# Sums of squares moved inside the first step of the next product, in three places of a two-block float32 network

## The chip, the cores and the metric

One core of one Trainium2 chip runs the whole program in one launch. The metric is the device time of one execution in microseconds (us); the median of several executions is compared.

## What is computed

The reference is two small transformer-like blocks, one after the other, on 512 tokens of width 1024, all in float32. Only the first block matters here. Its two layers each end in the same feed-forward part, and the second layer begins with a query projection:

```python
def rms_norm(x, g, eps=NORM_EPS):
    xf = x.astype(jnp.float32)
    y = xf * lax.rsqrt(jnp.mean(xf * xf, axis=-1, keepdims=True) + eps)
    return (y * g.astype(jnp.float32)).astype(x.dtype)

def swiglu_ffn(h, w_gu, w_down):
    gate, up = jnp.split(h @ w_gu, 2, axis=-1)
    return (jax.nn.silu(gate) * up) @ w_down
...
        h = rms_norm(x, g_ffn[layer])
        x = x + swiglu_ffn(h, ffn_w_gu[layer], ffn_w_down[layer])
```

The hidden width is 2816, that is 22 tiles of 128. Since the norm's factor is one number for each token, it can be multiplied in after the product: `(x*g) @ w` is formed from the residual stream x at once, and the factor 1/sqrt(mean(x*x) + eps) is needed only where the product's result is taken out of PSUM.

## The kernel before, in words

**Products.** x lies transposed, as 8 tiles of 128 features by 512 tokens. A float32 product is done as three matmuls in the type float32r: high part times high part, low times high, high times low (`three`, lines 2479 to 2481). The kernel works through a list of steps. A step of a product with 8 input tiles makes 256 output features in two PSUM banks with 8 x 2 x 3 = 48 matmuls of 128x128 by 512. Each step reads one weight slot of 128x2048 numbers. Slots go through two buffers by turns: SyncE fetches the raw weights (`fill`, two DMAs for a slot, let go when the low part of the slot two before it is done), ScalarE copies them to the type float32r (`high`, line 1220, `w_hi`), GpSimd subtracts to get the low part (`low`, line 1099, `w_lo`), in 8 pieces of 256 columns or, with `cut=False`, in one instruction. `high(n)` waits until the step that used slot n-2 is over.

**A product's input.** For each of the 8 tiles k VectorE multiplies x by the norm's gain into one of two buffers `xf` (L1800), ScalarE copies it to `X_hi` (L1242, `x_high1`), VectorE subtracts to get `X_lo` (L1773). The first step of the product waits at tile k for `X_lo` of tile k.

**Sums of squares.** Ahead of three products whose input is normed (gu0, q, gu1) ScalarE squares the 8 tiles of x into two buffers by turns (`norm_squares`, L1283), and TensorE sums over partitions by a plain float32 matmul with a 128x128 matrix of ones (`norm_sum`, L2555), which the profile shows as two passes for each tile. Square k waits for the sum of tile k-2. Before, all eight sums stand on TensorE ahead of the first step of the product. After the last of them ScalarE takes the root (L1285, `rt`) and VectorE the reciprocal (L1788).

**gu0 and gu1** (gate and up) have 22 steps each, written as a loop of 11 iterations with 2 steps, on each engine its own loop. When a step is over VectorE scales the two banks by `rt` (L1822, L1823), ScalarE applies Silu (L1205), VectorE multiplies (L1826), ScalarE copies the result to `hb_hi` (L1207), VectorE subtracts to get `hb_lo` (L1829). In ScalarE's loop (`ffn`) each step begins with `high` of the slot of the next step, then comes Silu and the copy of the step itself. In GpSimd's loop (`low_ffn`) the low parts are uncut. The loops of dn0 and dn1 (4 steps with 22 input tiles and 3 slots each) follow; on ScalarE they hold copies alone.

**q** has 4 steps in straight-line code. Beside its later steps TensorE does small matmuls for the heads, put between input tiles by a function `parts(k)` that `features` calls ahead of tile k: rotations of queries (L2859) and head sums (L2850). The first of them stands in step 1 ahead of tile 2 and needs step 0 scaled (`aq`, L2167), and VectorE waits for the table `rope` before it does that (L2210). SyncE issues the DMA of `rope` (L1051) after the fills of all four q slots. The fourth fill waits for the low part of the second slot.

**Order.** All orders are written out by hand, one instruction stream for each engine, tied by semaphores. TensorE works strictly in the order of its stream.

Of the kernel before, what the change touches and what calls it, by code (L numbers as in the profile page):

```python
# [19 lines left out]
ACT = mybir.ActivationFunctionType  # L20
# [5 lines left out]
KT = D // P  # L26
TT = S // P
F = 2816
FT = F // P
# [171 lines left out]
PL = make_plan()  # L201
# [372 lines left out]
def build(nc, t, out):  # L574
# [3 lines left out]
    with ctx:  # L578
# [25 lines left out]
        xf = sb("xf", [P, 2, S])  # L604
# [242 lines left out]
        def bank(i, n=S):  # L847
            return psum[:, i, 0:n]
# [4 lines left out]
        def wait_done(eng, key):  # L853

            eng.wait_ge(job_done, JB.info[key][2] + 1)
# [30 lines left out]
        def c_(name, n=P, o=0):  # L886
            return cst[:, CST[name] + o:CST[name] + o + n]
# [32 lines left out]
        def square_buffer(i):  # L920

            return (xf[:, :, :], pt8[:, 6:8, :], sgate[:, :, :], tq2[:, :, :])[i]
# [161 lines left out]
        def _(pool):  # L1084
# [24 lines left out]

            def low_ffn(layer):  # L1110
                n0 = PL.first_slot[f"gu{layer}"]
                with pool.Fori(0, FT // 2) as i:
                    for j in range(2):
                        low(n0 + j, 2 * i, cut=False)
                n0 = PL.first_slot[f"dn{layer}"]
                with pool.Fori(0, 2) as i:
                    for j in range(6):
                        low(n0 + j, 6 * i, cut=False)
# [71 lines left out]
        def _(act):  # L1190
# [7 lines left out]

            def ffn(layer):
                s0, n0 = PL.first[f"gu{layer}"], PL.first_slot[f"gu{layer}"]  # L1200
                with act.Fori(0, FT // 2) as i:
                    for j in range(2):
                        high(n0 + j + 1, 32 * i, 16 * i)
                        act.wait_ge(ff_raw, FT * layer + j + 1 + 2 * i)
                        act.activation(sgate[:, j, :], sgate[:, j, :], ACT.Silu).then_inc(ff_gate, 1)  # L1205
                        act.wait_ge(ff_prod, FT * layer + j + 1 + 2 * i)
                        act.activation(hb_hi[:, bass.ds(2 * i + j, 1), :], xf[:, j:j + 1, :],  # L1207
                                       ACT.Copy).then_inc(ff_hi, 1)
                n0 = PL.first_slot[f"dn{layer}"]
                with act.Fori(0, 2) as i:  # L1210
                    for j in range(6):
                        high(n0 + j + 1, 96 * i, 44 * i)
# [20 lines left out]
            def x_high1(v, k, src=None):  # L1233
                if src is None:
                    act.wait_ge(xf_ready, xf_count(v, k))
                if v:
                    act.wait_ge(kstep, xv_last_k(v - 1, k))
                if src is None:
                    f = mixed_at(k) if v < XV["y"] else xf[:, k % 2, :]
                else:  # L1240
                    f = src[:, k, :]
                act.activation(X_hi[:, k, :], f, ACT.Copy).then_inc(xhi_ready, 1)  # L1242
# [24 lines left out]
                    if after is not None:  # L1267
                        after(k)

            def norm_squares(i, v=None):  # L1270

                for k in range(0 if v is None else 6):
                    x_high1(v, k)
                for k in range(KT):
                    if k >= 6 and v is not None:
                        x_high1(v, k)
                    if i == 0:
                        wait_job(act, ("xt", k))
                    elif k % 2 == 0:
                        wait_step(act, PL.first[("", "o", "dn0", "ao")[i]] + k // 2)  # L1280
                    if k >= 2:
                        act.wait_ge(sq_used, 7 * i + k - 1)
                    act.activation(square_buffer(i)[:, k % 2, :], x[:, k, :], ACT.Square).then_inc(sq_ready, 1)  # L1283
                wait_done(act, ("rms", i))
                act.activation(rt[:, :], bank(6), ACT.Sqrt, bias=cst[:, C_EPS6:C_EPS6 + 1],  # L1285
                               scale=1.0 / D).then_inc(job_a, 1)
# [260 lines left out]
            for i in range(4):  # L1547
                if PL.first_slot["o"] + 1 + i < len(PL.slots):
                    high(PL.first_slot["o"] + 1 + i)
            norm_squares(1, XV["ffn0"])  # L1550
            ffn(0)
            act.wait_ge(lam_row, 1)
            wait_done(act, ("lam",))
            act.activation(col[:, 0:2], psum[:, 7, 0:2], ACT.Exp).then_inc(job_a, 1)
            norm_squares(2, XV["qin"])
            rq, rk = xf[0:16, 1, :], xf[0:16, 0, :]

            def qk_part(n):
# [19 lines left out]
                        act.activation(n_hi[:, :], rk, ACT.Copy).then_inc(kn_h, 1)  # L1578

            for n in range(72):  # L1580
                if n % 8 == 0:
                    next_slot(PL.first["q"] + n // 8)
                if n == 24:
                    x_high(XV["kvin"])
                qk_part(n)
# [14 lines left out]
            for p in range(N_UNITS + 2):  # L1600
                j = p // PER_STEP
# [38 lines left out]
                x_high1(XV["attn"], k, oT)  # L1640
            for i in range(PL.count["ao"]):
                next_slot(PL.first["ao"] + i)
            norm_squares(3, XV["ffn1"])
            ffn(1)

            for k in range(KT):
# [820 lines left out]
        def _(pe):  # L2467
            order = [0]

            def begin(key):  # L2470
                assert JB.order[order[0]] == key, (JB.order[order[0]], key)
                order[0] += 1
                wait_banks(pe, key)
                return job_banks(key)[0]
# [39 lines left out]
            def ffn(layer):  # L2514

                s0, v = PL.first[f"gu{layer}"], XV[f"ffn{layer}"]
                with pe.Fori(0, FT // 2) as i:
                    for j in range(2):
                        pe.wait_ge(step_d, PL.taken[s0 + j][1] - 2 + 2 * i)
                        features(s0 + j, v if j == 0 else None, dyn=2 * i, check=False)  # L2520
                s0 = PL.first[f"dn{layer}"]
                with pe.Fori(0, 2) as i:
                    for j in range(2):
                        pe.wait_ge(step_d, PL.taken[s0 + j][1] - 2 + 2 * i)
                        features(s0 + j, None, hb_hi, hb_lo, dyn=6 * i, check=False,
                                 tile_ready=(ff_lo, FT * layer) if j == 0 else None)
# [21 lines left out]
                for i in range(PL.count[name]):  # L2548
                    (kind or features)(PL.first[name] + i, v if i == 0 else None)

            def norm_sum(i):
                begin(("rms", i))
                for k in range(KT):
                    pe.wait_ge(sq_ready, 8 * i + k + 1)
                    ins = pe.matmul(bank(6), c_("ones"), square_buffer(i)[:, k % 2, :], start=k == 0, stop=k == KT - 1)  # L2555
                    ins.then_inc(sq_used if k < KT - 1 else job_done, 1)

            pe.wait_ge(cst_in, 16)
            for k in range(KT):
# [2 lines left out]
                for tt in range(TT):  # L2562
                    ins = pe.transpose(psum[:, b, P * tt:P * tt + P], xtok[:, tt, P * k:P * k + P], c_("ident"))
                ins.then_inc(job_done, 1)
            norm_sum(0)
            pe.wait_ge(rows_in, 16 * (len(ROWS_A) + len(ROWS_B) + 2))
            b = begin(("pv",))
            pe.transpose(psum[:, b, 0:P], prow[0][:, :], c_("ident"))
# [241 lines left out]
            for k in range(KT):  # L2810
# [8 lines left out]
                if k % 2 == 0:  # L2819
# [4 lines left out]
                    for m in range(2):  # L2824
# [5 lines left out]
                                    (sg_hi[96:128, 1, :], sg_lo[96:128, 1, :]), False, True)  # L2830
                    ins.then_inc(kstep, 1)
            product("o", XV["y"])
            norm_sum(1)
            ffn(0)
            pe.wait_ge(lam_row, 1)
            b = begin(("lam",))
            pe.matmul(psum[:, b, 0:2], cst[0:1, CST["ones"]:CST["ones"] + P], col[0:1, 14:16], start=True,
                      stop=True).then_inc(job_done, 1)
            norm_sum(2)

            def qk_part(n):
                for what, w, i in QK_AT.get(n, ()):
# [32 lines left out]
                two(bank(b), heads_r[:, P * k:P * k + P], (n_hi[:, :], n_lo[:, :])).then_inc(job_done, 1)  # L2875

            for i in range(4):
                features(PL.first["q"] + i, XV["qin"] if i == 0 else None, parts=lambda k: qk_part(8 * i + k))
            pe.wait_ge(rt_ready, 3)
            b = begin(("rtT",))  # L2880
            for tt in range(TT):
# [106 lines left out]
                b = begin(("oinv", k))  # L2988
                two(bank(b), heads_r[:, P * k:P * k + P], (n_hi[:, :], n_lo[:, :])).then_inc(job_done, 1)
            product("ao", XV["attn"])  # L2990
            norm_sum(3)
            ffn(1)
            def to_tokens(n, k):

# [203 lines left out]
```

## Time and profile before

| | us |
|---|---|
| median of three executions | 2226.78 (2226.38 to 2231.42) |
| the profiled execution, its own time | 2220.09 |
| its span, from the first to the last instruction | 2218.3 |
| TensorE busy (PE) | 2005.0, 90% |
| VectorE (DVE), ScalarE (ACT), GpSimd (POOL) busy | 792.4, 812.1, 777.7 |
| low parts of the weights on GpSimd, 588 instructions | 706.1 |
| mean granted TensorE clock | 0.948 of 2.4 GHz |

The profile calls the engines PE (TensorE's matmuls), PEld (its weight loads, which overlap), DVE, ACT, POOL and SP. Shares of busy time are means over stages with different limits. Matmuls are pipelined, so two that follow each other overlap in the rows, and a stream is best read by the distance from one start to the next.

### The profile page before, as it was taken

To read this page: it belongs to the slowest core of one execution; us is meant where nothing else is said; L and a number is where in the kernel's file an instruction comes from. 1 tells how busy PE (TensorE), PEld (TensorE's weight loads), DVE (VectorE), ACT (ScalarE), POOL (GpSimd) and SP (SyncE) were. 2 spreads that over 40 slices of the span, in tenths; PEclk is the share of its full clock that TensorE was granted. 3 is DMA by queue.
4 is the path that set the end of the run, shared out by engine and by line. 5 is a ranking of instruction groups with operands and counts; after the bars stand their busy time and mean duration, and the time that the engine had idled before them with its cause. 6 is when DMAs were issued, how large, how long until landed. Compare 5 with 4: busy or idle time off the path is not lost.

```text
span 2218.3 us, 37433 instructions
## 1 busy us (share of the span) xinstructions
PE 2005.0 (90%) x15948; PEld 1570.5 (71%) x15948; DVE 792.4 (36%) x1248; ACT 812.1 (37%) x1061; POOL 777.7 (35%) x644
## 2 busy tenths in 40 slices
PE   5997976668999999989999899999999999979987
PEld 3666866643778888866667478888887886768767
DVE  5586443324332221014766632222102223324333
ACT  6766133332244343122247534343312423242232
POOL 3353322210334443433432034444444433234432
PEclk8998999986899999999999899999999999989988
DMA  5111000010223333222121022333223121131211
GB/s 154 57 50 63 2 5 5 4 48 23 59 75 94 99 90 109 95 80 67 65 69 39 0 76 76 97 92 102 97 91 106 60 77 57 39 100 58 77 38 58
DMA packets 190138, 147.16 MB, mean 66 GB/s; under 512 B 6826, under 2 KB 188289, under 8 KB 190004
## 3 DMA queue, kind: packets, MB, share of 16 engines
q1 hardware_dynamic: 190004, 145.18, 21.2%
q8 instruction: 107, 1.75, 0.3%
q14 instruction: 27, 0.22, 0.0%
HBM read 143.07 MB, written 2.10 MB: 65 GB/s over the span
## 4 chain that ended last, share of the span: by engine, by line
PE 79%; DVE 7%; ACT 5%; issue 5%; POOL 2%; DMA 1%; SPq 0%; DVEq 0%; ACTq 0%
PE psum L2479 21%; PE psum L2481 20%; PE psum L2480 20%; PE psum L2634 4%; POOL w_lo L1099 2%; ACT w_hi L1220 1%; DVE X_lo L1773 1%; PE psum L2555 1%; PE psum L2485 1%; PE psum L2859 1%; PE psum L2920 1%; PE psum L2933 1%; PE psum L2850 1%; PE psum L3030 1%; DVE col L2230 0%
## 5 line engine op out<-in xcount | busy, mean ns | idle before, releaser
L1099 POOL TENSOR_TENSOR w_lo<-weight_raw,w_hi 128x256 fp32r<-128x256 f32 (+5 forms) x588 | 706.1, 1233 | 1236.5 <-ACT w_hi L1220 1236.4
L2479 PE MATMUL psum<-X_hi,w_hi 128*128 128x512 f32 x1400 | 577.4, 412 | 26.3 <-DVE X_lo L1773 17.8
L2481 PE MATMUL psum<-X_hi,w_lo 128*128 128x512 f32 x1400 | 552.3, 395 | 0.0
L2480 PE MATMUL psum<-X_lo,w_hi 128*128 128x512 f32 x1400 | 551.9, 394 | 0.0
L1220 ACT ACTIVATE w_hi<-weight_raw 128x2048 fp32r<-128x2048 f32 (+2 forms) x134 | 249.5, 1862 | 362.9 <-PE psum L2481 338.3
L2479 PEld LDWEIGHTS psum<-X_hi,w_hi 128*128 128x128 f32 x1400 | 266.5, 190 | 126.8 <-issue 53.8
L2480 PEld LDWEIGHTS psum<-X_lo,w_hi 128*128 128x128 f32 x1400 | 266.8, 191 | 58.7 <-issue 7.5
L2481 PEld LDWEIGHTS psum<-X_hi,w_lo 128*128 128x128 f32 x1400 | 266.3, 190 | 58.1
L2479 PE MATMUL psum<-w_hi,X_hi 128*128 128x256 f32 x640 | 191.4, 299 | 13.0 <-DVE X_lo L1773 10.8
L2480 PE MATMUL psum<-w_lo,X_hi 128*128 128x256 f32 x640 | 185.1, 289 | 0.0
L2481 PE MATMUL psum<-w_hi,X_lo 128*128 128x256 f32 x640 | 184.9, 289 | 0.0
L1822 DVE TENSOR_TENSOR sgate<-rt,psum 128x512 f32<-128x512 f32 x44 | 30.3, 688 | 320.5 <-PE psum L2481 320.5
L2479 PEld LDWEIGHTS psum<-w_hi,X_hi 128*128 128x128 f32 x640 | 127.2, 199 | 21.0 <-issue 19.0
L2479 PE MATMUL psum<-hb_hi,w_hi 128*128 128x512 f32 x352 | 136.9, 389 | 0.0
L2480 PE MATMUL psum<-hb_lo,w_hi 128*128 128x512 f32 x352 | 136.9, 389 | 0.0
L2481 PE MATMUL psum<-hb_hi,w_lo 128*128 128x512 f32 x352 | 136.9, 389 | 0.0
L2480 PEld LDWEIGHTS psum<-w_lo,X_hi 128*128 128x128 f32 x640 | 127.0, 198 | 0.6 <-issue 0.5
L2481 PEld LDWEIGHTS psum<-w_hi,X_lo 128*128 128x128 f32 x640 | 126.7, 198 | 0.0
L1205 ACT ACTIVATE sgate<-sgate 128x512 f32<-128x512 f32 x44 | 27.9, 634 | 255.3 <-DVE sgate L1822 255.3
L1812 DVE TENSOR_TENSOR x<-x,psum 128x512 f32<-128x512 f32 x32 | 20.5, 682 | 224.6 <-PE psum L2481 224.6
L2480 PEld LDWEIGHTS psum<-hb_lo,w_hi 128*128 128x128 f32 x352 | 66.1, 188 | 13.8
L2481 PEld LDWEIGHTS psum<-hb_hi,w_lo 128*128 128x128 f32 x352 | 66.1, 188 | 13.8
(465 smaller groups left out, 2566.3 us busy)
## 6 DMA issues: line engine op xcount, KB each, us to landing
weight_raw<-in_ffn_w_gu SPq DMA_DIRECT2D x88, 512.0 KB, 4.8
weight_raw<-in_l_w_in SPq DMA_DIRECT2D x45, 512.0 KB, 4.7
weight_raw<-in_ffn_w_down SPq DMA_DIRECT2D x40, 512.0 KB, 3.6
weight_raw<-in_kv_w SPq DMA_DIRECT2D x16, 512.0 KB, 4.5
weight_raw<-in_l_w_out SPq DMA_DIRECT2D x16, 512.0 KB, 4.5
weight_raw<-in_rw_w_k SPq DMA_DIRECT2D x8, 512.0 KB, 6.6
weight_raw<-in_rw_w_r SPq DMA_DIRECT2D x8, 512.0 KB, 4.0
weight_raw<-in_rw_w_v SPq DMA_DIRECT2D x8, 512.0 KB, 4.0
```

Of the source, the lines that this page charges most:

```text
L1099: ins = pool.tensor_tensor(l, r, h.bitcast(F32), ALU.subtract)
L1205: act.activation(sgate[:, j, :], sgate[:, j, :], ACT.Silu).then_inc(ff_gate, 1)
L1220: last = act.activation(h, r, ACT.Copy)
L1773: dve.tensor_tensor(X_lo[:, k, :], f, X_hi[:, k, :].bitcast(F32), ALU.subtract).then_inc(xlo_ready, 1)
L1822: dve.tensor_tensor(sgate[:, j, :], rt[:, :], bank(b[0]), ALU.mult).then_inc(ff_raw, 1)
L2479: pe.matmul(ps, wh, xh, start=start, stop=False, skip_group_check=True)
L2480: pe.matmul(ps, wh, xl, start=False, stop=False, skip_group_check=True)
L2481: return pe.matmul(ps, wl, xh, start=False, stop=stop, skip_group_check=True)
L2485: pe.matmul(ps, w, xx[0], start=True, stop=False, skip_group_check=True)
L2555: ins = pe.matmul(bank(6), c_("ones"), square_buffer(i)[:, k % 2, :], start=k == 0, stop=k == KT - 1)
L2634: ins = pe.matmul(out(q, r, k), left(q, r, k), right(q, r, k), start=True, stop=True, skip_group_check=True)
L2850: ins = pe.matmul(psum[0:16, job_banks(key)[0], :], c_("sel64", 16, 16 * i), oT[:, i, :], start=i == first, stop=i == last)
```

## The change

In all three places (gu0, q, gu1) the eight sums leave their place ahead of the product. `features` gets them as `parts` of the first step: ahead of input tile k (k from 1) TensorE does the sum of tile k-1, and ahead of tile 7 those of tiles 6 and 7. On ScalarE squares and copies of input tiles take turns from the first tile on (before, six copies came first), and the copy `high` of the product's second weight slot moves from behind the root to between square 5 and tile 6. For that the first two steps of gu0 and gu1 are taken out of the loops of TensorE, ScalarE and GpSimd and written straight, the loops run from 1 to 10, and the low parts of these two slots are done in pieces. VectorE's loop stays as it is. The diff:

```diff
             def low_ffn(layer):
                 n0 = PL.first_slot[f"gu{layer}"]
-                with pool.Fori(0, FT // 2) as i:
+                low(n0)
+                low(n0 + 1)
+                with pool.Fori(1, FT // 2) as i:
                     for j in range(2):
                         low(n0 + j, 2 * i, cut=False)
...
-                with act.Fori(0, FT // 2) as i:
+
+                def hidden(j, at_, dyn):
+                    act.wait_ge(ff_raw, FT * layer + j + 1 + dyn)
+                    act.activation(sgate[:, j, :], sgate[:, j, :], ACT.Silu).then_inc(ff_gate, 1)
+                    act.wait_ge(ff_prod, FT * layer + j + 1 + dyn)
+                    act.activation(hb_hi[:, at_, :], xf[:, j:j + 1, :], ACT.Copy).then_inc(ff_hi, 1)
+
+                hidden(0, slice(0, 1), 0)
+                high(n0 + 2)
+                hidden(1, slice(1, 2), 0)
+                with act.Fori(1, FT // 2) as i:
                     for j in range(2):
                         high(n0 + j + 1, 32 * i, 16 * i)
-                        act.wait_ge(ff_raw, FT * layer + j + 1 + 2 * i)
...
+                        hidden(j, bass.ds(2 * i + j, 1), 2 * i)
...
-            def norm_squares(i, v=None):
-
-                for k in range(0 if v is None else 6):
-                    x_high1(v, k)
+            def norm_squares(i, v=None, early=None):
+
                 for k in range(KT):
-                    if k >= 6 and v is not None:
+                    if v is not None:
                         x_high1(v, k)
...
+                    if k == 5 and early is not None:
+                        high(early)
...
-            norm_squares(1, XV["ffn0"])
+            norm_squares(1, XV["ffn0"], PL.first_slot["gu0"] + 1)
...
-            norm_squares(2, XV["qin"])
+            norm_squares(2, XV["qin"], PL.first_slot["q"] + 1)
...
-                if n % 8 == 0:
+                if n % 8 == 0 and n:
                     next_slot(PL.first["q"] + n // 8)
...
-                with pe.Fori(0, FT // 2) as i:
+                pe.wait_ge(step_d, PL.taken[s0][1] - 2)
+                features(s0, v, check=False, parts=norm_beside(1 + 2 * layer))
+                pe.wait_ge(step_d, PL.taken[s0 + 1][1] - 2)
+                features(s0 + 1, check=False)
+                with pe.Fori(1, FT // 2) as i:
...
+            def norm_part(i, k):
+
+                if k == 0:
+                    begin(("rms", i))
+                pe.wait_ge(sq_ready, 8 * i + k + 1)
+                pe.matmul(bank(6), c_("ones"), square_buffer(i)[:, k % 2, :], start=k == 0, stop=k == KT - 1
+                          ).then_inc(sq_used if k < KT - 1 else job_done, 1)
+
+            def norm_beside(i):
+
+                def part(k):
+                    if k:
+                        norm_part(i, k - 1)
+                    if k == KT - 1:
+                        norm_part(i, k)
+                return part
...
-                features(PL.first["q"] + i, XV["qin"] if i == 0 else None, parts=lambda k: qk_part(8 * i + k))
+                features(PL.first["q"] + i, XV["qin"] if i == 0 else None,
+                         parts=norm_beside(2) if i == 0 else lambda k: qk_part(8 * i + k))
```

The calls `norm_sum(1)`, `norm_sum(2)` and `norm_sum(3)` are gone.

## Rows read from the trace of the kernel before

**Rows 1.** The page's part 4: the chain that ended last, by engine
```profile
PE 79%; DVE 7%; ACT 5%; issue 5%; POOL 2%; DMA 1%; SPq 0%; DVEq 0%; ACTq 0%
```

**Rows 2.** Timeline of PE before gu0: start, length, line, tiles [idle before <-releaser]
```profile
611.92 0.39 PE L2481 MATMUL psum<-X_hi,w_lo 128*128 128x512 f32 x1
613.91 7.85 PE L2555 MATMUL psum<-pt,cst 128*128 128x512 f32 x16 [1.60 <-ACT pt L1283]
...
621.83 0.40 PE L2480 MATMUL psum<-X_lo,w_hi 128*128 128x512 f32 x1
```

**Rows 3.** Timeline of DVE at the start of gu0
```profile
622.52 3.35 DVE L1788 RECIPROCAL rt<-rt 128x512 f32<-128x512 f32 x1 [1.73 <-ACT rt L1285]
632.70 0.69 DVE L1822 TENSOR_TENSOR sgate<-rt,psum 128x512 f32<-128x512 f32 x1 [6.83 <-PE psum L2481]
...
654.46 0.69 DVE L1822 TENSOR_TENSOR sgate<-rt,psum 128x512 f32<-128x512 f32 x1 [7.17 <-PE psum L2481]
...
665.61 0.69 DVE L1822 TENSOR_TENSOR sgate<-rt,psum 128x512 f32<-128x512 f32 x1 [7.45 <-PE psum L2481]
```

**Rows 4.** Waits in gu0 and dn0, 615 to 990: total, times, longest (us)
```profile
PEld psum L2479 <- POOL w_lo L1099: 4.0, 10, 0.4
```

**Rows 5.** Timeline of ACT at the start of gu0
```profile
621.79 0.69 ACT L1285 ACTIVATE rt<-psum,cst 128x512 f32<-128x512 f32 x1 [1.22 <-PE psum L2555]
...
646.46 1.28 ACT L1220 ACT_TABLE_LOAD   x1
```

**Rows 6.** Timeline of POOL in gu0: low parts of slots 2 and 3
```profile
637.47 4.59 POOL L1099 TENSOR_TENSOR w_lo<-weight_raw,w_hi 128x2048 fp32r<-128x2048 f32 x1 [7.07 <-ACT w_hi L1220]
649.75 4.60 POOL L1099 TENSOR_TENSOR w_lo<-weight_raw,w_hi 128x2048 fp32r<-128x2048 f32 x1 [7.68 <-ACT w_hi L1220]
```

**Rows 7.** Timeline of PE between dn0 and q
```profile
983.48 0.38 PE L2837 MATMUL psum<-col,cst 1*128 1x2 f32 x2
991.86 10.44 PE L2555 MATMUL psum<-sgate,cst 128*128 128x512 f32 x16 [8.00 <-ACT sgate L1283]
```

**Rows 8.** Timeline of DVE between dn0 and q
```profile
985.96 0.69 DVE L1773 TENSOR_TENSOR X_lo<-xf,X_hi 128x512 fp32r<-128x512 f32 x1 [30.09 <-ACT X_hi L1242]
...
1018.46 1.28 DVE L2167 TENSOR_TENSOR aq<-rt,psum 128x512 f32<-128x512 f32 x2 [9.79 <-DMA rope<-c_rope]
```

**Rows 9.** Timeline of ACT between dn0 and q: copy of q's second slot
```profile
1003.02 1.91 ACT L1220 ACTIVATE w_hi<-weight_raw 128x2048 fp32r<-128x2048 f32 x1
```

**Rows 10.** Timeline of POOL between dn0 and q: low part of that slot
```profile
1005.01 5.59 POOL L1099 TENSOR_TENSOR w_lo<-weight_raw,w_hi 128x256 fp32r<-128x256 f32 x8 [21.99 <-ACT w_hi L1220]
```

**Rows 11.** Timeline of PE in q: a 128x128 float32 matmul between a step's matmuls
```profile
1037.16 0.40 PE L2481 MATMUL psum<-X_hi,w_lo 128*128 128x512 f32 x1
1037.39 1.02 PE L2859 MATMUL psum<-aq,rotg 128*128 128x512 f32 x2
...
1038.49 0.39 PE L2480 MATMUL psum<-X_lo,w_hi 128*128 128x512 f32 x1
```

**Rows 12.** Timeline of PE in q: a 128x16 float32 matmul between a step's matmuls
```profile
1041.66 0.40 PE L2481 MATMUL psum<-X_hi,w_lo 128*128 128x512 f32 x1
...
1043.29 0.40 PE L2480 MATMUL psum<-X_lo,w_hi 128*128 128x512 f32 x1
```

**Rows 13.** ACT by line in gu0's loop, 621 to 866: busy, mean ns
```profile
L1220 ACT ACT_TABLE_LOAD x11 | 14.1, 1283 | 0.2
L1205 ACT ACT_TABLE_LOAD x11 | 14.1, 1283 | 0.2
```

**Rows 14.** ACT by line in dn0's loop, 866 to 983, its first group
```profile
L1220 ACT ACTIVATE w_hi<-weight_raw 128x2048 fp32r<-128x2048 f32 (+1 forms) x12 | 21.3, 1774 | 89.4 <-PE psum L2481 89.4
```

**Rows 15.** Stretches: length, PE, PEld, DVE, ACT, POOL, granted clock, DMA, GB/s
```profile
987.40:997.60 10.20, 5.74 (x7) 2.42 (x8) 6.39 (x12) 4.81 (x9) 0.00 (x0) 0.50 0.00 1
1693.70:1696.10 2.40, 0.03 (x1) 0.06 (x1) 2.05 (x3) 0.00 (x0) 2.12 (x3) 1.00 0.00 0
...
1697.30:1700.70 3.40, 3.40 (x10) 2.63 (x9) 0.00 (x0) 0.00 (x0) 0.00 (x0) 0.50 0.91 294
```

More of the change, by code:

```diff
@@ L1200, in ffn @@
                 s0, n0 = PL.first[f"gu{layer}"], PL.first_slot[f"gu{layer}"]
-                with act.Fori(0, FT // 2) as i:
+                def hidden(j, at_, dyn):
[7 more added lines that the diff above has]
+                with act.Fori(1, FT // 2) as i:
                     for j in range(2):
                         high(n0 + j + 1, 32 * i, 16 * i)
-                        act.wait_ge(ff_raw, FT * layer + j + 1 + 2 * i)
[L1205 to L1208, printed above, removed]
+                        hidden(j, bass.ds(2 * i + j, 1), 2 * i)
                 n0 = PL.first_slot[f"dn{layer}"]
@@ L1642, in _ @@
                 next_slot(PL.first["ao"] + i)
-            norm_squares(3, XV["ffn1"])
+            norm_squares(3, XV["ffn1"], PL.first_slot["gu1"] + 1)
             ffn(1)
@@ L2516, in ffn @@
                 s0, v = PL.first[f"gu{layer}"], XV[f"ffn{layer}"]
-                with pe.Fori(0, FT // 2) as i:
+                pe.wait_ge(step_d, PL.taken[s0][1] - 2)
[3 more added lines that the diff above has]
+                with pe.Fori(1, FT // 2) as i:
                     for j in range(2):
                         pe.wait_ge(step_d, PL.taken[s0 + j][1] - 2 + 2 * i)
-                        features(s0 + j, v if j == 0 else None, dyn=2 * i, check=False)
+                        features(s0 + j, dyn=2 * i, check=False)
                 s0 = PL.first[f"dn{layer}"]
@@ L2549, in product @@
                     (kind or features)(PL.first[name] + i, v if i == 0 else None)
[L2551 to L2556, printed above, removed]
+            def norm_part(i, k):
[11 more added lines that the diff above has]
+                return part
             pe.wait_ge(cst_in, 16)
@@ L2564, in _ @@
                 ins.then_inc(job_done, 1)
-            norm_sum(0)
+            for k in range(KT):
+                norm_part(0, k)
             pe.wait_ge(rows_in, 16 * (len(ROWS_A) + len(ROWS_B) + 2))
@@ L2832, in _ @@
             product("o", XV["y"])
-            norm_sum(1)
             ffn(0)
@@ L2838, in _ @@
                       stop=True).then_inc(job_done, 1)
-            norm_sum(2)
             def qk_part(n):
@@ L2990, in _ @@
             product("ao", XV["attn"])
-            norm_sum(3)
             ffn(1)
```

## The prediction, on record before the change was run

> **What bounds the kernel now.** I read the chain that ended last first: TensorE holds 79% of it [rows 1], so a change pays where TensorE stands still or does work that could lie elsewhere. Then its timeline around the three places. Ahead of gu0 the last matmul of the product before starts at 611.92, the sums follow after 1.60 us of idling, and the first step runs from 621.6 (its second matmul starts at 621.83, one spacing of 0.23 after that) [rows 2]. The place ahead of gu1 looks the same to within 0.1 us. A step is 10.88 us long: VectorE takes out step 0 at 632.70 and step 2 at 654.46, two steps later [rows 3]; so a tile of 6 matmuls is 1.36 and a spacing 0.227. Inside gu0 each second step starts late: 665.61 to 654.46 is 11.15, that is 0.27 more, and the waits show TensorE held 10 times by the low part of a weight slot [rows 4]. Between dn0 and q TensorE stands for 8.00 us and then does the sums in 10.44 [rows 7]; but what q then waits for is the table rope: VectorE starts on step 0's result at 1018.46, after idling 9.79 for that DMA [rows 8]. So three stages have three different limits, and each part below is costed at its own.
>
> **A sum inside a step.** The sums are not removed, they are put between tiles. The nearest row is a float32 matmul of the same shape (128x128 weights, 512 columns) already between float32r matmuls: 1037.16 to 1038.49 is 1.33, less two spacings, 0.88 [rows 11]. With 16 weight columns it is 1.63 less 0.45, 1.18 [rows 12]. I take 0.88, the row of the same shape, and keep 1.18 as the upper bound. Nothing cheaper is seen: in the block each took (621.60 - 613.91)/8 = 0.96, with waits for squares among it [rows 2].
>
> **gu0 and gu1.** Step 0 then starts right behind the last matmul, at 612.15, and ends 10.88 + 8 x 0.88 = 17.9 later, at 630.05; before, 621.6 + 10.88 = 632.48. That is 2.4 gained for TensorE. But the norm's factor comes later against the step: the eighth sum is done one tile before the end, at 628.69. Root and reciprocal follow as before (the root starts 0.19 behind the sum and takes 0.69 [rows 5], the reciprocal 3.35 [rows 3]): 632.96. With about 0.1 for entering VectorE's loop, which was covered until now, step 0 is taken out from 633.06, against 632.70 before. This is the new wait: behind it hang, in order, Silu, the copy to `hb_hi`, ScalarE's copy of slot 2, which stands behind them in its stream, and GpSimd's low part of slot 2, and step 2 needs that. From taking out to the end of the low part was 632.70 to 642.06, 9.36 [rows 3, 6]. So the low part ends at 642.42 and step 2 starts 0.16 later (as step 3 did behind the low part ending at 654.35 [rows 6], 654.51 being 665.61 less 10.88 and the 0.22 from a step's end to its taking out). Step 2: 642.58, before 643.36. Of 2.4 only 0.8 is left there. At step 3, before 654.51 and now 642.58 + 10.88 = 653.46, it is 1.05, since its low part is no longer last.
>
> **Table loads in the loop.** Before, each of the 11 iterations on ScalarE loads an activation table twice, ahead of the first copy and ahead of Silu, 1283 ns each [rows 13], although the second half of an iteration copies behind Silu with no load. In dn0's loop, entered from Silu's table and holding only copies, there is none [rows 14]. What differs is that gu0's loop is entered behind a root and repeated behind Silu, dn0's always behind Silu. I read this as: a load stands where the ways in bring different tables. With the first two steps written straight, the loop is entered behind Silu as well, and I expect its 20 loads to go, one load for Silu staying ahead of step 0, under the reciprocal. The load at the loop's head (646.46 [rows 5]) lies on the path to the odd slots: 654.46 less 10.88 is 643.58, and from there to 654.35 it is 10.77, as against 9.36 without. Without it the low part comes 1.3 earlier than needed, and 9 further waits of 0.27 go: 2.4. For each of gu0 and gu1 1.05 + 2.4 = 3.5, together 7.0.
>
> The Trainium skill says otherwise ("ScalarE activation tables: per-element evaluation and per-set limits", section "Table sets in the compiler and the runtime"): "The back end places the table loads per block: greedy longest run". By that a loop's body starts over and would keep a load at its head. The rows speak against it twice, two loads in one body and none in the other. By this rule the gain of this part would be the first 1.05 each.
>
> **q.** TensorE is free at 983.86 [rows 7], the first `X_lo` is there at 986.65 [rows 8], so step 0 starts at 986.7, 2.8 us behind. After such a gap the clock may fall: behind an idle stretch of 2.40 us the granted clock was 0.50, 1.2 GHz, for 3.40 us, while the matmuls already ran [rows 15]. I take the same here, a loss of 1.7; both ends are kept, none and twice that. The fourth sum ends 4 x (1.36 + 0.88) = 8.95 later, with the loss at 997.35; square 5 waits for it, and behind that square ScalarE copies q's second slot, at 998.1. Before it was 1003.02 [rows 9]: 4.9 earlier. The low part follows in 5.59 [rows 10]; two `X_lo` now fall beside it, for which I allow 0.2, so 4.7. Behind the low part SyncE lets go the fourth fill and then rope, both issued by the same queue and landing as before; so step 0 is taken out 4.7 earlier, at 1013.8, and with it all of q. The factor is no limit there: eighth sum at 1004.9, with root, reciprocal and 2.2 us of small VectorE work 1011.4. Step 0 itself ends at 1006.3, 6.7 us earlier than before, and TensorE waits ahead of the first rotation longer than before: most of that goes into this wait.
>
> **Edits costed at nothing.** Two slots' low parts in pieces take 5.6 and not 4.6 each. The first ends near 609.1, before step 0 needs it at 612.15. The second starts behind the early copy at 623.8 and ends at 629.4 to 629.9 with two `X_lo` between; step 1 needs it at 630.05, and the wait of 1.65 at step 2 covers what is late. Tile 6 of x is copied behind the early copy: `X_lo` at 625.1, needed at 625.57; without this slack of 0.5 each tenth late moves the factor and step 2. A square waits for the sum two tiles back and the next tile's copy waits behind it, 2.1 us in all, while TensorE needs 4.5 for two tiles and sums: covered twice over. SyncE's fills are let go earlier, never later.
>
> **Sum.** 7.0 + 4.7 = 11.7. The profiled execution of 2220.1 would become 2208.4. It is 6.7 below the median of 2226.8, from which I take the same off: **2215.1**.
>
> **Rivals.**
> The loads stay in the loop. For it speaks only that I infer the rule from two loops. Gain 2 x 1.05 + 4.7 = 6.8, time 2220.0. Chance 0.13.
> A sum costs 1.18. Each of gu0 and gu1 loses 8 x 0.3 = 2.4 on the way to step 2 and keeps 1.1; q loses 4 x 0.3 and keeps 3.5. Gain 5.7, time 2221.1. Chance 0.10.
> The clock stays high in q. TensorE starts at 986.7, and 1.7 more comes back: 2213.4. Chance 0.12.
> Slower: the clock stays low through q's first step, as it did for 10.2 us around the sums before [rows 15], in which TensorE stood half the time. The eighth sum then ends 16.5 later than in my sum without a loss, at 1019.8, the factor and the small work at 1026.2, not rope, decide, and q loses 7.7 against before, more than the 7.0 won elsewhere: 2227.5. It decides from 31.5 us of low clock on, where half of that puts the factor 7.0 behind 1018.46. Against it: in a stream without holes 3.4 us were enough to come back [rows 15]. Chance 0.05.
>
> **How the numbers follow.** The forecast has 0.57, and 0.03 is left for what I don't see, taken as slower. Bounds: 2213.4 with the clock high, 2221.1 with dear sums; executions of one kernel differ by 1 to 2, so the range is 2212 to 2222. About 0.3%, 6.7 us, is what a measurement here can tell from no change. Faster by more: nearly all of the forecast (0.54), all of the high clock (0.12), half of the loads' rival (0.07): 0.73. Within it: the rest of the forecast, the other half, dear sums, and most of the low clock: 0.23. Slower: 0.04.
>
> **What would show it.** Right: no PE rows of L2555 in one block; in gu0 step 0 taken out near 633 less the shift, step 2 a wait of some 1.7 behind `w_lo`, no further waits of 0.27, and one table load, not 22, for each of gu0 and gu1 on L1205 and L1220; in q `aq` still behind rope, and some 30 us, not 34.6, behind the end of TensorE's last matmul of that stretch, `lam` (L2837, 983.86). Wrong: loads at L1220 in the loop; a sum of over 1 us between tiles; `aq` behind the factor; a low clock after q's first step has begun for more than 7 us.

## The result and the profile after

The changed kernel took 2217.25 us (median of 14 runs, 2212.15 to 2224.65), the kernel before, run beside it on the same chips, 2228.3 (14 runs, 2222.28 to 2238.35). The ratio is 0.9943, with a 95% interval of 0.9929 to 0.9957: about 12.7 us, or 0.57%, faster (the two medians by themselves differ by 11.05). The forecast was a gain of 11.7 and a time of 2215.1.

The profiled execution of after took 2218.33 us with a span of 2216.2, only 1.8 less than the one of before. That is no contradiction: the two executions also differ where the code does not. I cut each span at events that both have, VectorE's residual adds and the first `aq`, and took the differences of their starts:

| stretch, us | before | after | less |
|---|---|---|---|
| start to the residual add of step 2 of the product before gu0 | 601.47 | 613.48 | -12.01 |
| from there to the same add in dn0 (gu0, dn0) | 352.21 | 348.71 | 3.50 |
| from there to the first `aq` (q's first step) | 64.78 | 59.69 | 5.09 |
| from there to the add of step 2 ahead of gu1 | 292.72 | 290.39 | 2.33 |
| from there to the same add in dn1 (gu1, dn1) | 352.61 | 348.72 | 3.89 |
| from there to the end | 554.52 | 555.24 | -0.72 |

Rows two, three and five hold the change: 12.5 together. The first row is not the change's: over all profiled executions of both kernels and of the experiments that stretch lay between 600.9 and 616.75, with the same code. So the whole time says little of a few microseconds, and the stretches say much: the same kernel profiled again gave 348.69, 59.79, 290.57 and 348.71 for the four in the middle. The experiments below are read by these stretches, with the whole time beside them.

The page of after, its part 1 and its chain of work by engine (for [rows 1]): TensorE's busy time fell from 2005.0 to 1993.2 for the same 15948 matmuls (the mean granted clock was 0.954 and not 0.948, and busy time times clock is the same to 0.1%, so that fall needs no other cause), ScalarE's from 812.1 to 754.3, which is 42 table loads of 1.28 and a little more, and GpSimd has 28 instructions more.

```profile
PE 1993.2 (90%) x15948; PEld 1570.1 (71%) x15948; DVE 790.1 (36%) x1248; ACT 754.3 (34%) x1019; POOL 786.9 (36%) x672
...
PE 75%; issue 7%; DVE 7%; ACT 5%; POOL 4%; DMA 1%; SPq 0%; DVEq 0%; ACTq 0%; POOLq 0%
```

**gu0.** In after the lines stand 8 lower (L1830 is the old L1822, L1228 the old L1220). Times of after are 12.01 later than those of before up to this point. TensorE's timeline, where [rows 2] had one block of sums: start, length, line, tiles, [idle before, releaser].

```profile
625.29 0.39 PE L2489 MATMUL psum<-X_hi,w_lo 128*128 128x512 f32 x1
625.52 1.02 PE L2568 MATMUL psum<-pt,cst 128*128 128x512 f32 x2
...
626.60 0.39 PE L2488 MATMUL psum<-X_lo,w_hi 128*128 128x512 f32 x1
...
642.43 0.47 PE L2487 MATMUL psum<-X_hi,w_hi 128*128 128x512 f32 x1 [0.20 <-POOL w_lo L1099]
...
654.50 0.50 PE L2487 MATMUL psum<-X_hi,w_hi 128*128 128x512 f32 x1 [0.90 <-POOL w_lo L1099]
```

The sum lies between two tiles of step 0. Step 1 starts at 642.43 and step 2 at 654.50, each behind a low part. VectorE's timeline there, for [rows 3], shows what followed: the reciprocal, then step 0 to step 4 taken out.

```profile
641.61 3.35 DVE L1796 RECIPROCAL rt<-rt 128x512 f32<-128x512 f32 x1 [3.37 <-ACT rt L1293]
645.18 0.69 DVE L1830 TENSOR_TENSOR sgate<-rt,psum 128x512 f32<-128x512 f32 x1 [0.23 <-DVE rt L1796]
...
653.64 0.69 DVE L1830 TENSOR_TENSOR sgate<-rt,psum 128x512 f32<-128x512 f32 x1 [4.82 <-PE psum L2489]
...
665.71 0.69 DVE L1830 TENSOR_TENSOR sgate<-rt,psum 128x512 f32<-128x512 f32 x1 [8.46 <-PE psum L2489]
...
676.59 0.69 DVE L1830 TENSOR_TENSOR sgate<-rt,psum 128x512 f32<-128x512 f32 x1 [7.17 <-PE psum L2489]
...
687.47 0.69 DVE L1830 TENSOR_TENSOR sgate<-rt,psum 128x512 f32<-128x512 f32 x1 [7.17 <-PE psum L2489]
```

From step 2 on every step is 10.88 long; the 0.27 at each second one is gone. Of the ten waits for a low part of [rows 4] these are left, in the view of waits in gu0 and dn0, 627 to 990 (total, times, longest); they are the starts of steps 1 and 2 just shown:

```profile
PEld psum L2487 <- POOL w_lo L1099: 1.3, 1, 1.3
PE psum L2487 <- POOL w_lo L1099: 1.1, 2, 0.9
```

ScalarE's timeline and GpSimd's, for [rows 5] and [rows 6]: the early copy, root, the one table load, copy of slot 2; low parts of slots 0, 1 and 2.

```profile
633.84 1.90 ACT L1228 ACTIVATE w_hi<-weight_raw 128x2048 fp32r<-128x2048 f32 x1
...
640.88 0.69 ACT L1293 ACTIVATE rt<-psum,cst 128x512 f32<-128x512 f32 x1 [2.46 <-PE psum L2568]
641.59 1.28 ACT L1206 ACT_TABLE_LOAD   x1
...
647.87 1.90 ACT L1228 ACTIVATE w_hi<-weight_raw 128x2048 fp32r<-128x2048 f32 x1
...
615.53 7.52 POOL L1099 TENSOR_TENSOR w_lo<-weight_raw,w_hi 128x256 fp32r<-128x256 f32 x8 [5.29 <-ACT w_hi L1228]
635.81 6.47 POOL L1099 TENSOR_TENSOR w_lo<-weight_raw,w_hi 128x256 fp32r<-128x256 f32 x8 [12.76 <-ACT w_hi L1228]
649.85 4.59 POOL L1099 TENSOR_TENSOR w_lo<-weight_raw,w_hi 128x2048 fp32r<-128x2048 f32 x1 [7.57 <-ACT w_hi L1228]
```

**q.** The timelines of PE, ACT, POOL, SP and DVE in the order of the chain (for [rows 7] to [rows 10]): the end of `lam`, TensorE's start, the copy of q's second slot, its low part, the DMA of rope, the first `aq`, TensorE's first rotation.

```profile
992.00 0.38 PE L2859 MATMUL psum<-col,cst 1*128 1x2 f32 x2
995.32 0.48 PE L2487 MATMUL psum<-X_hi,w_hi 128*128 128x512 f32 x1 [2.94 <-DVE X_lo L1781]
...
1006.73 1.90 ACT L1228 ACTIVATE w_hi<-weight_raw 128x2048 fp32r<-128x2048 f32 x1
...
1008.70 6.47 POOL L1099 TENSOR_TENSOR w_lo<-weight_raw,w_hi 128x256 fp32r<-128x256 f32 x8 [17.16 <-ACT w_hi L1228]
...
1016.16 0.50 SPq L1051 DMA_DIRECT2D rope<-c_rope  x1
...
1021.88 1.28 DVE L2175 TENSOR_TENSOR aq<-rt,psum 128x512 f32<-128x512 f32 x2 [2.42 <-issue]
...
1023.22 1.22 PE L2880 MATMUL psum<-aq,rotg 128*128 128x512 f32 x1 [4.92 <-DVE aq L2175]
```

`lam` ends at 992.38, and `aq` starts 29.50 behind it; before it was 1018.46 less 983.86, 34.60. For the wait of 2.42 ahead of `aq` this profile names no releaser. That it is rope follows from the experiments: `aq` comes 5.7 to 5.9 behind the issue of rope in every run that has it in this place (6.87 in the one profile of before), and 2.4 earlier when rope is issued sooner.

### The profile page after: what moved, and what is told of

The parts are those of the page before. It is cut to its first block, busy times and chain, and to the rows that moved or that the text cites. A ratio compares the mean times of both kernels' runs of the same rounds, so it can differ in the third digit from the quotient of the medians.

```text
span 2216.2 us, 37365 instructions
## 1 busy us (share of the span) xinstructions
PE 1993.2 (90%) x15948; PEld 1570.1 (71%) x15948; DVE 790.1 (36%) x1248; ACT 754.3 (34%) x1019; POOL 786.9 (36%) x672
## 4 chain that ended last, share of the span: by engine, by line
PE 75%; issue 7%; DVE 7%; ACT 5%; POOL 4%; DMA 1%; SPq 0%; DVEq 0%; ACTq 0%; POOLq 0%
PE psum L2487 20%; PE psum L2489 19%; PE psum L2488 19%; PE psum L2657 4%; POOL w_lo L1099 4%; ACT w_hi L1228 2%; DVE X_lo L1781 1%; PE psum L2493 1%; PE psum L2942 1%; PE psum L2880 1%; PE psum L2955 1%; PE psum L2871 1%; PE psum L3051 1%; DVE col L2238 0%; PE psum L2494 0%
## 5 line engine op out<-in xcount | busy, mean ns | idle before, releaser
L1099 POOL TENSOR_TENSOR w_lo<-weight_raw,w_hi 128x256 fp32r<-128x256 f32 (+4 forms) x616 | 715.3, 1192 | 1215.9 <-ACT w_hi L1228 1215.7
L1228 ACT ACTIVATE w_hi<-weight_raw 128x2048 fp32r<-128x2048 f32 (+2 forms) x134 | 249.2, 1860 | 355.8 <-PE psum L2489 329.8
L1830 DVE TENSOR_TENSOR sgate<-rt,psum 128x512 f32<-128x512 f32 x44 | 30.2, 687 | 299.3 <-PE psum L2489 298.9
L2487 PEld LDWEIGHTS psum<-hb_hi,w_hi 128*128 128x128 f32 x352 | 66.1, 188 | 13.8
```

Source lines behind the costliest of these rows:

```text
L1099: ins = pool.tensor_tensor(l, r, h.bitcast(F32), ALU.subtract)
L1228: last = act.activation(h, r, ACT.Copy)
L1830: dve.tensor_tensor(sgate[:, j, :], rt[:, :], bank(b[0]), ALU.mult).then_inc(ff_raw, 1)
L2487: pe.matmul(ps, wh, xh, start=start, stop=False, skip_group_check=True)
```

## The experiments

**A Silu ahead of the loop, in the kernel before.** My theory was that a table load stands in ScalarE's loop only because the loop is entered behind a root and repeated behind Silu. If so, a single activation of Silu ahead of the unchanged loop must take the loads out of it; by the rival each body keeps its loads. The edit, for gu0 and gu1:

```diff
+                act.activation(ypart[:, 0:1], cst[:, C_EPS6:C_EPS6 + 1], ACT.Silu)
                 with act.Fori(0, FT // 2) as i:
```

> The kernel before with one Silu on a column of 128 numbers ahead of ScalarE's loop of gu0 and of gu1, nothing else; it makes both ways into the loop bring Silu's table. Theory (a load stands where the ways in bring different tables): of 44 loads in the two loops none is left, one for Silu stays ahead of each; the 10 late starts of 0.27 us in each of gu0 and gu1 go, 5.4 us in all, ratio to before 0.9976. Rival (loads are placed for each loop body from new): 11 or 22 loads stay in each loop, the late starts stay, ratio 1.000.

Measured: 2222.09 us, ratio 0.9967 (0.9943 to 0.9991). The stretch with gu0 took 349.47 (before 352.21), that with gu1 349.51 (before 352.61): 2.7 and 3.1 less. ScalarE by line in gu0, 620 to 870, for [rows 13]:

```profile
L1206 ACT ACTIVATE sgate<-sgate 128x512 f32<-128x512 f32 x21 | 13.3, 634 | 146.2 <-DVE sgate L1823 146.2
...
L1201 ACT ACT_TABLE_LOAD x1 | 1.3, 1283 | 0.0
```

One load, at the new line; of the 22 in the loop none is left, and with them went all of TensorE's waits for low parts in gu0. One instruction of 0.2 us does what I had put down to the steps written straight.

**A root ahead of the loop, in the changed kernel.** The reverse: the loop from 1 to 10 is entered behind a root again.

```diff
+                act.activation(ypart[:, 0:1], cst[:, C_EPS6:C_EPS6 + 1], ACT.Sqrt)
                 with act.Fori(1, FT // 2) as i:
```

> The changed kernel with one square root on a column of 128 numbers ahead of ScalarE's loop of gu0 and of gu1, so that the ways in bring different tables again. Theory: 20 loads come back on each of the two lines in each loop pair (10 iterations, 2 loads), the 9 or 10 late starts of 0.27 in each loop come back, about 5.2 us lost against the changed kernel, ratio to before 0.9966. Rival (the gain does not hang on the loads): ratio as the changed kernel's, 0.9943.

Measured: 2220.75 us, ratio to before 0.9961 (0.9943 to 0.998). The stretches grew by 2.94 and 3.31 against after, 6.2 together; 5.2 were expected. ScalarE by line, 612 to 866, and TensorE's waits, 612 to 975:

```profile
L1206 ACT ACT_TABLE_LOAD x11 | 14.1, 1283 | 0.2
...
L1229 ACT ACT_TABLE_LOAD x10 | 12.8, 1283 | 0.2
```
```profile
PEld psum L2488 <- POOL w_lo L1099: 5.5, 11, 1.3
```

The loads are back, and so are the waits (the longest, 1.3, is the one of step 2, which after has too). What is above the expectation: by the starts of VectorE's taking out, the first of the ten late steps, which has the added root and its own load on its way, is late by 0.45 in gu0 and 0.46 in gu1, and the nine others by 0.27 to 0.28 in gu0 but 0.30 to 0.34 in gu1. This run also tells what the sums inside the step are worth while the loads stay: against before, gu0 is 0.57 shorter and gu1 0.59, the added root's 0.2 included. The two runs together settle the table loads: the steps written straight matter because they change the way into the loop.

**The second slot copied behind the root again.** This asks whether the early copy is what makes sums inside a step pay.

```diff
-                    if k == 5 and early is not None:
-                        high(early)
...
+                if early is not None:
+                    high(early)
```

> The changed kernel with the copy of the product's second weight slot put back behind the root. Theory: the sums inside the step need the early copy. In gu0 and gu1 the low part of slot 1 then ends near 25 us behind the start of step 0 and not 18, step 1 starts 6.7 later, of which 1.2 is got back at step 2: 5.5 lost in each. In q the low part, the last fill and rope come 6.9 later. Together 18 lost against the changed kernel, so slower than before by 5: ratio 1.0025. Rival (the copy is covered anyway): 0.9943.

Measured: 2239.06 us, ratio to before 1.0041 (1.0023 to 1.0058): slower than before. Against after, gu0 lost 8.46, gu1 8.61 and q 7.82, 24.9 in all; I had expected 18. TensorE's timeline at the end of step 0, and stretches of it (length, busy time of PE, PEld, DVE, ACT, POOL, granted clock, DMA share, GB/s):

```profile
634.09 0.40 PE L2489 MATMUL psum<-X_hi,w_lo 128*128 128x512 f32 x1
642.25 0.77 PE L2487 MATMUL psum<-X_hi,w_hi 128*128 128x512 f32 x1 [7.76 <-POOL w_lo L1099]
642.81 0.63 PE L2488 MATMUL psum<-X_lo,w_hi 128*128 128x512 f32 x1
```
```profile
642.30:646.60 4.30, 4.30 (x10) 3.40 (x11) 0.00 (x0) 0.00 (x0) 4.30 (x1) 0.50 0.76 214
646.90:652.00 5.10, 5.10 (x24) 4.18 (x23) 0.00 (x0) 0.00 (x0) 0.00 (x0) 1.00 0.81 217
```

The hole is 7.76 long, and behind it the granted clock was 0.50, 1.2 GHz, for 4.3 us more, with the matmuls running: 2.15 lost that no expectation had. gu1 has the same hole of 7.76, and from 1358.8 to 1363.1 the same 0.50. Besides, step 1 starts 7.57 later than in after (36.52 behind the residual add and not 28.95), where 6.7 were expected; with 2.15 more and 1.2 got back at step 2 this is 8.5. q's 0.9 above its 6.9 is something else, since its stretch ends at `aq`, which waits for rope and not for TensorE: the granted clock was low for 5.5 us of q's first step (0.50 from 996.1 to 1001.6) and not for 3.4, so the sums and the root ahead of the copy came 1.1 later. (Behind q's hole of 6.86, too, it was 0.50 for 4.3, but that lies behind the issue of rope.) So the copy between square 5 and tile 6 is no small thing beside the sums: without it the change loses.

**Both slots' low parts in one instruction.** In the prediction the pieces stood among the edits costed at nothing.

```diff
-                low(n0)
-                low(n0 + 1)
+                low(n0, cut=False)
+                low(n0 + 1, cut=False)
```

> The changed kernel with the low parts of the first two slots of gu0 and gu1 in one instruction each. Theory: X_lo of tile 6 falls into the one of slot 1 and waits for its end, 3.8 us; tiles 6 and 7, the last sums, the factor and step 2 all come 3.8 later, in gu0 and in gu1: 7.6 lost, ratio 0.9977. Rival (the pieces only cost time on GpSimd, 4.6 and not 6.5 us, and the wait is covered): 0.994 or a little less.

Measured: 2228.63 us, ratio to before 0.999 (0.9972 to 1.0008). gu0 lost 6.38 and gu1 5.07 against after, 11.4, and with that nearly all the gain; 7.6 were expected. The timelines of POOL, DVE and PE in gu0's first step:

```profile
629.26 4.53 POOL L1099 TENSOR_TENSOR w_lo<-weight_raw,w_hi 128x2048 fp32r<-128x2048 f32 x1 [15.65 <-ACT w_hi L1228]
...
609.46 4.70 DVE L1781 TENSOR_TENSOR X_lo<-xf,X_hi 128x512 fp32r<-128x512 f32 x1 [0.33 <-ACT X_hi L1250]
...
629.73 5.21 DVE L1781 TENSOR_TENSOR X_lo<-xf,X_hi 128x512 fp32r<-128x512 f32 x2 [2.75 <-ACT X_hi L1250]
...
634.39 0.79 PE L2487 MATMUL psum<-X_hi,w_hi 128*128 128x512 f32 x1 [3.19 <-DVE X_lo L1781]
634.98 0.63 PE L2488 MATMUL psum<-X_lo,w_hi 128*128 128x512 f32 x1
635.41 0.63 PE L2489 MATMUL psum<-X_hi,w_lo 128*128 128x512 f32 x1
```
```profile
631.20:634.30 3.10, 0.01 (x1) 0.00 (x0) 3.10 (x2) 0.63 (x1) 2.59 (x1) 0.90 0.00 0
634.90:640.60 5.70, 5.70 (x11) 3.06 (x10) 0.04 (x1) 0.00 (x0) 0.00 (x0) 0.51 0.68 187
```

An `X_lo` is 0.69 long elsewhere. Those of tiles 6 and 7 are one row here, 5.21 long, beside a subtraction on GpSimd that ends at 633.79. One `X_lo` by itself beside such a subtraction, the row at 609.46, took 4.70 and ended 0.55 behind it (the low part of slot 0 ran from 608.98 to 613.61). With pieces the one of tile 6 took 0.82 in after. TensorE stands 3.19 for it here, and again a stretch of low clock follows, 5.7 long here with spacings of 0.43 instead of 0.23. That is the excess in gu0, 2.6 above the 3.8; gu1, whose stretch of low clock was shorter (0.50 from 1340.2 to 1343.6), has 1.3. The pieces are not free cover, they carry the change.

**q put back.** Only q's part undone: six copies first, the slot behind the root, the sums ahead of the step.

```diff
-            norm_squares(2, XV["qin"], PL.first_slot["q"] + 1)
+            norm_squares(2, XV["qin"])
...
-                if n % 8 == 0 and n:
+                if n % 8 == 0:
...
+            for k in range(KT):
+                norm_part(2, k)
...
-                         parts=norm_beside(2) if i == 0 else lambda k: qk_part(8 * i + k))
+                         parts=lambda k: qk_part(8 * i + k))
```

> The changed kernel with q as before: eight sums ahead of its first step, six tiles copied ahead of the squares, the second slot copied behind the root. Theory: 5.1 us lost against the changed kernel (the trace has the first taking out of q 29.9 us behind the end of dn0 and not 35.0), ratio to before 0.9966. Rival (q's gain is given back later in q, where TensorE waits ahead of the first rotation 4.9 and not 3.9): under 1 us lost, 0.9945.

Measured: 2216.15 us, ratio to before 0.9959 (0.9938 to 0.998). The whole time can't tell it from after. The stretch can: 63.72 against 59.69, so 4.03 lost, with gu0 and gu1 as in after (348.73 and 348.72). It is 1.1 less than the 5.1 read from the two first profiles. SyncE and VectorE tell why. First the issue of rope in the timeline of before (its `aq` is in [rows 8]), then issue and `aq` of this run; the order of the code is the same:

```profile
1011.59 2.13 SPq L1051 DMA_DIRECT2D rope<-c_rope  x1
```
```profile
1007.63 0.50 SPq L1051 DMA_DIRECT2D rope<-c_rope  x1
...
1013.35 1.29 DVE L2177 TENSOR_TENSOR aq<-rt,psum 128x512 f32<-128x512 f32 x2 [8.63 <-DMA rope<-c_rope]
```

From issue to `aq` it is 6.87 in the profile of before and 5.72 here; in after and the runs above 5.7 to 5.9. The one profiled execution of before had a slow issue (2.13 instead of 0.50). The run with a Silu ahead, which has before's code in q, took 63.34 for the stretch. So 3.6 to 4.0 of q's 5.1 belong to the change. TensorE's wait ahead of the first rotation is 2.72 here and 4.92 in after: 2.2 of what TensorE wins ahead of it goes into this wait.

**The third slot copied ahead of Silu.** After the change step 2 waits, and behind step 0's taking out stood Silu, the copy of `hb_hi` and only then the copy of slot 2. If that order is the limit, a swap must give back about what these cost.

```diff
-                hidden(0, slice(0, 1), 0)
                 high(n0 + 2)
+                hidden(0, slice(0, 1), 0)
```

> The changed kernel with the copy of slot 2 of gu0 and gu1 ahead of step 0's Silu on ScalarE, which waits there for the factor. Theory (step 2 waits only for the chain behind the late factor): the copy starts when step 0 ends, low part of slot 2 done near 6.6 us behind that, the wait of 1.2 ahead of step 2 goes in gu0 and in gu1: 2.3 won, ratio 0.9933. Rival (Silu and its copy, now 2 us later against the copy of slot 2, push slot 3 and step 1's work): nothing won, 0.9943.

Measured: 2211.05 us, ratio to before 0.9932 (0.991 to 0.9953). gu0 and gu1 are each 1.21 shorter than after (347.50 and 347.51). Of TensorE's waits for low parts in gu0 and dn0 (620 to 975) one is left, that of step 1:

```profile
PE psum L2487 <- POOL w_lo L1099: 0.2, 1, 0.2
```

So the wait of step 2 is the limit of that stretch, as the prediction had it. q was 1.49 shorter too, with the same code there: the clock stayed up (see the last section).

**Rope ahead of the fourth fill.** If rope is what q waits for, and it is late only because it stands behind a fill that waits for a low part, then moving it one place up frees `aq` until the factor is last.

```diff
-            fill_product("q")
+            for i in range(3):
+                fill(PL.first_slot["q"] + i)
...
+            fill(PL.first_slot["q"] + 3)
```

> The changed kernel with the DMA of rope ahead of the fill of q's fourth slot in SyncE's stream. Theory (rope sets the first taking out in q): rope lands long before it is needed, the factor and the small work behind it become last, taking out 2.4 us earlier, TensorE's wait ahead of the first rotation 2.5 and not 4.9; ratio 0.9932. Rival (the factor is as late, or the fourth slot is then late): 0.9943 or slower.

Measured: 2207.68 us, ratio to before 0.9916 (0.9894 to 0.9938). q's stretch is 57.29, 2.40 less than after. Rope is issued at 998.86, 12.4 behind the end of `lam` instead of 23.8, and `aq` follows the factor and VectorE's small work:

```profile
1008.56 3.35 DVE L1798 RECIPROCAL rt<-rt 128x512 f32<-128x512 f32 x1 [3.37 <-ACT rt L1295]
...
1013.56 1.28 DVE L2177 TENSOR_TENSOR aq<-rt,psum 128x512 f32<-128x512 f32 x2
```

**Both.** The last two edits together, once by themselves and once on another chip beside the changed kernel again.

> The changed kernel with both: slot 2 copied ahead of step 0's Silu, rope ahead of the last fill. Theory: the two are apart in time and add up, 4.7 us won against the changed kernel, ratio to before 0.9922. Rival (one of them gives nothing): 0.9933.

Measured: 2203.07 us, ratio to before 0.9898 (0.9873 to 0.9923); gu0 and gu1 347.52 and 347.51, q 55.68.

> The changed kernel as it is, beside the next one on the same chip. Both theories: ratio to before 0.9943, as on record.

Measured: 2215.91 us, ratio 0.9944 (0.9925 to 0.9963).

> Slot 2 copied ahead of step 0's Silu and rope ahead of the last fill, once more, beside the changed kernel itself. Theory (both waits were on the path, and the stages of the earlier profiles, 1.2 less in gu0, 1.2 less in gu1, 2.4 to 4.0 less up to the first taking out in q, come through to the end): 4.8 to 6.4 less than the changed kernel, 0.9915 to 0.992 of before. Rival (given back later): the changed kernel's time.

Measured: 2206.77 us, ratio 0.9909 (0.9889 to 0.993), beside 2227.29 of before and 2215.91 of after on that chip. It is faster than both, by 9.1 against after, more than the 4.8 to 6.4 expected. The stretches with gu0, q and gu1 account for 1.2 + 4.1 + 1.2 of it. Some 1.4 lie between `aq` and the end of the product ahead of gu1 (289.02 and 288.96 in the two runs, against 290.1 to 291.8 in all others of the changed kernel's family). That is the clock too: TensorE does the same 1357 matmuls there, busy 274.99 us at a mean granted clock of 0.97, against 276.53 at 0.96 in the profile of after beside it. Why the clock stayed up longer is not shown. And 1.5 of q's 4.1 is the clock that stayed up, as in the run with the third slot first.

## Why the prediction was right

The mechanism of each part was as forecast; I go through its steps, with times of after less the 12.01.

**The sum inside a step, 0.88.** Tiles with a sum follow each other at 2.24 (the first sums start at 625.52 and 627.76), that is 1.36 + 0.88. Dear sums at 1.18 are out.

**gu0's first steps, 0.8 and 1.05.** The factor: the reciprocal ends at 644.96, less 12.01 that is 632.95 (forecast 632.96). Step 0 taken out: 633.17 (633.06; entering VectorE's loop cost 0.23, not 0.1). Low part of slot 2: ends at 642.43 (642.42; the way there was 0.1 shorter, which hid that). Step 2 starts at 642.49 (642.58), 0.87 earlier than before, and step 3 is taken out 1.03 earlier. Of the 2.4 that the sums had cost ahead of the step most of the rest lies in step 2's wait, shown by the 1.2 that the third slot's earlier copy gave back.

**Table loads, 2.4.** 3.50 less 1.03 leaves 2.47 for the nine later steps. Taken alone, the load's removal was worth 2.7 and 3.1, its return 2.9 and 3.3. The Trainium skill's sentence quoted in the prediction ("ScalarE activation tables: per-element evaluation and per-set limits", section "Table sets in the compiler and the runtime") would have kept a load in the body: the run with one Silu ahead, one load and 22 copies with none, goes against it in this kernel.

**gu1, 3.5.** 3.89 measured. In after, and in the run with a Silu ahead, the stretches of gu0 and gu1 agree to 0.04; before's own differ by 0.40, and so do those of the run with a root ahead, by 0.38. So with the loads in the loop gu1 is the longer one, and it is not one execution's chance: before's ten late steps are late by 0.27 to 0.28 in gu0 and by 0.29 to 0.33 in gu1. The prediction took gu0's 0.27 for both. Why a late step costs more in gu1 is open.

**q, 4.7.** The profiles gave 5.1, of which 3.6 to 4.0 hold against the two runs with q as before. Counted from the end of `lam`: TensorE starts at 2.94 (2.84), the clock falls for 3.4 us as assumed, the copy of the second slot starts at 14.35 (14.24). The step that failed is the allowance of 0.2 for two `X_lo` beside the low part: it took 6.47 and not 5.8, and ends at 22.79 (22.02). Rope is issued 0.99 behind it, as before. The missing 0.7 was covered up in the first comparison by the slow rope of before's profile, on whose 6.87 I had built. The factor's end was right: small work done at 27.08 (27.5), 2.4 ahead of `aq`, which waits for rope. And the time went where I said: TensorE waits 4.92 ahead of the first rotation, against 2.72 in the run with q put back and 3.87 in before's profile with its slow rope:

```profile
1019.80 2.07 PE L2859 MATMUL psum<-aq,rotg 128*128 128x512 f32 x2 [3.87 <-DVE aq L2167]
```

That, and 0.4 that step 1 waits for its low part, is why 6.7 at the step's end became 4 to 5.

**Edits costed at nothing.** The first slot's low part ended at 611.04, 1.9 later than I had it (7.52 for the pieces, not 5.6), 1.1 ahead of its need at 612.15. The second ended at 630.27, 0.4 to 0.9 late, and made step 1 0.45 late; step 2's wait covered that. So nothing was lost, with most of the slack used up. What I underrated is what the cover is worth: one instruction in place of the pieces costs 11.4.

**The sum.** By stretches 3.5 + 3.9 + 4.0 = 11.4 (11.0 with 3.6 for q), by the profiles 12.5, by whole times 12.7 (2228.3 x 0.0057) with an interval of 9.6 to 15.8, against 11.7. That it came so near is in part luck: gu1 gave 0.4 more than forecast and q 0.7 to 1.1 less. And the prediction took executions of one kernel to differ by 1 to 2, while the 14 runs of after spread over 12.5. Most of what gu0 and gu1 gave is not the moved sums' own: the Silu ahead alone, with the sums where they were, won 5.8 of the 7.4, and after is 0.76 and 0.79 shorter than that run. In the table between `aq` and the end of the product ahead of gu1 2.33 more seems to be won; the run with the Silu ahead, which has before's code there, took 290.16, so it is before's execution that was long (a mean granted clock of 0.95 there and 0.96 in after, with 278.67 and 276.33 us of TensorE for the same 1357 matmuls). Of the rivals, loads that stay and dear sums are refuted; a clock that stays high did not come in after, but in runs with the third slot first; a clock low through q's first step came in none.

## What to carry over

When work is moved into a step, follow the result of that work to whoever needs it two steps on: here most of TensorE's gain went into a new wait, and without the early copy of the second slot the move lost. In this kernel a loop on ScalarE that was entered from another table than its body's last one had its loads on every turn; one activation ahead of it took them out, and that was worth more than moving the sums in gu0 and gu1. And where unchanged stages move by more than the change is worth, compare stretches between events that both traces have.

## What the runs showed that I had not expected

A hole costs twice. Behind holes of 7.76 and 3.19 us in the runs above the granted clock stayed at 1.2 GHz for 4.3 and 5.7 us of running matmuls. Behind q's gap of 2.9 us it did not always fall, with the same code from there on. The same 3.4 us, first in after, then with the third slot first:

```profile
995.60:999.00 3.40, 3.40 (x9) 2.29 (x7) 2.26 (x5) 0.92 (x2) 0.00 (x0) 0.51 0.05 14
```
```profile
986.50:989.90 3.40, 3.40 (x14) 2.45 (x14) 2.29 (x5) 2.03 (x4) 0.00 (x0) 1.00 0.06 19
```

14 matmuls instead of 9. Half the clock for 3.4 us costs 1.7 at most, near the 1.49 by which these q stretches differ. It fell in the profiles of after (both) and of the runs with a root ahead, the slot late, the parts uncut and rope first. It stayed up in all three with the third slot first, an edit some 350 us ahead whose own wait was long over. So neat a split of six and three comes by chance once in 84 draws, but it was looked for afterwards; whether the edit and the clock are linked, and how, is open: no run tests it.

VectorE and GpSimd hinder each other both ways. An `X_lo` of 0.69 took 4.70 beside GpSimd's uncut subtraction, until 0.55 behind its end, and beside pieces 0.82 to 1.23. The eight pieces took 5.59 with VectorE idle (in after, from 985.94) and 5.59 too beside a reciprocal [rows 10], but 6.47 beside two `X_lo` and 7.52 beside three `X_lo` and the multiplications between them.

And one execution's DMA is one sample: 6.87 us from rope's issue to its use in the profile of before, 5.7 to 5.9 in eight others.
